# Moving the first turn of expert rows ahead of a top-k search, in a two-layer hybrid decoder kernel

## What is computed

```python
def peer(h, wq, keys, u_tab, v_tab):
    q = (xc @ wq).reshape(c, PEER_HEADS, 2, PEER_QDIM // 2)
    sc = jnp.einsum('thpd,hpkd->thpk', q, keys)
    top_v, top_i = lax.top_k(sc, PEER_TOPK)
    cand = (top_v[:, :, 0, :, None] + top_v[:, :, 1, None, :]).reshape(c, PEER_HEADS, -1)
    best_v, best_pos = lax.top_k(cand, PEER_TOPK)
    ids = jnp.take_along_axis(cand_id, best_pos, axis=-1)
    gate = jax.nn.softmax(best_v, axis=-1)
    act = jax.nn.gelu(jnp.einsum('td,thkd->thk', xc, u_tab[ids])) * gate
    return jnp.einsum('thk,thkd->td', act, v_tab[ids])

for layer in range(2):
    x = x + mixed(rms_norm(x, norm_mix[layer])) @ w_out[layer]
    x = x + peer(rms_norm(x, norm_ffn[layer]), ...)
```

## Time and profile before

| | us |
|---|---|
| median of 3 runs | 1578.69 (1577.34 to 1579.03) |
| the profiled execution | 1583.69 |
| its span in the profile | 1581.9 |
| PE busy | 1366.8 |
| DVE busy | 1173.6 |
| ACT busy | 455.0 |
| POOL busy | 608.3 |

### The profile page before, as it was taken

The page is one execution under the profiler, slowest core; times in us unless marked ns, Lnnn a source line. Parts: engine busy times, 40 slices in busy tenths (PEclk is TensorE's granted clock), DMA queues, the critical chain, the costliest instruction groups (busy, mean ns, idle before and its releaser), DMA issues.

```text
span 1581.9 us, 15174 instructions
## 1 busy us (share of the span) xinstructions
PE 1366.8 (86%) x4622; PEld 741.3 (47%) x4622; DVE 1173.6 (74%) x2848; ACT 455.0 (29%) x1095; POOL 608.3 (38%) x525
## 2 busy tenths in 40 slices
PE   8998999999695997988888799999969787788777
PEld 4766455554472444443356345455437433333333
DVE  6828999788698887874569788886658987665554
ACT  3522144443212234342122134343212222121112
POOL 1003355345334334553434333545434434333331
PEclk9999999999898999998989899999989889989999
DMA  9648999999999999999999999999999999999997
GB/s 360 269 164 347 389 380 422 406 402 421 423 421 421 422 398 422 422 419 423 423 410 409 422 423 420 417 384 403 422 423 419 388 408 422 422 419 421 422 421 300
DMA packets 87517, 629.97 MB, mean 398 GB/s; under 512 B 9825, under 2 KB 11105, under 8 KB 16910
## 3 DMA queue, kind: packets, MB, share of 16 engines
q0 software_dynamic: 74144, 537.97, 82.6%
q1 hardware_dynamic: 13294, 91.05, 14.1%
HBM read 627.91 MB, written 1.06 MB: 398 GB/s over the span
## 4 chain that ended last, share of the span: by engine, by line
PE 43%; DMA 29%; DVE 18%; issue 7%; ACT 3%; POOL 1%; SPq 0%; DVEq 0%; ACTq 0%
DMA ring<-table_uv,ids 28%; PE ps L1669 24%; DVE ring L1301 6%; PE ps L1636 5%; PE ps L1449 3%; PE ps L1412 2%; PE ps L1614 1%; ACT acts L797 1%; ACT diag L820 1%; PE ps L1516 1%; PE ps L1680 1%; POOL ring L1724 1%; DVE W L1276 1%; DVE W L1274 1%; DVE W L1277 1%
## 5 line engine op out<-in xcount | busy, mean ns | idle before, releaser
L1669 PE MATMUL ps<-ring,diag 128*128 128x512 f32 x1884 | 890.0, 627 | 194.3 <-ACT diag L820 185.4
L1724 POOL DMA_INDIRECT ring<-table_uv,ids x512 | 602.7, 1177 | 939.1 <-PE ps L1669 779.4
L1669 PEld LDWEIGHTS ps<-ring,diag 128*128 128x128 f32 x1884 | 370.7, 201 | 663.6 <-issue 652.0
L1301 DVE CUSTOM_DVE_ANT_0 ring<-ring,h 128x1024 f32<-128x1024 f32 x384 | 455.2, 1223 | 139.9 <-DMA ring<-table_uv,ids 137.9
L797 ACT ACTIVATE acts<-dots,small 128x4 f32<-128x4 f32 x126 | 37.5, 297 | 876.3 <-DVE dots L1301 850.3
L1301 DVE CUSTOM_DVE_ANT_0 ring<-ring,ps 128x1024 f32<-128x1024 f32 x120 | 144.6, 1220 | 97.7 <-DMA ring<-table_uv,ids 97.5
L820 ACT ACTIVATE diag<-cst,weights 128x128 f32<-128x128 f32 x471 | 151.4, 390 | 28.9 <-DVE weights L1310 27.8
L1449 PE MATMUL ps<-W,hT 128*128 128x512 f32 (+2 forms) x256 | 95.2, 527 | 2.7 <-DVE hT L940 2.7
L1636 PEld LDWEIGHTS ps<-hT,W 128*128 128x128 f32 x832 | 94.5, 192 | 3.3 <-issue 3.3
L1636 PE MATMUL ps<-hT,W 128*128 128x128 f32 x832 | 95.3, 275 | 0.0
L1449 PEld LDWEIGHTS ps<-W,hT 128*128 128x128 f32 x256 | 48.5, 190 | 52.0 <-issue 47.4
(11 more groups left out here) (316 smaller groups left out, 1190.8 us busy)
## 6 DMA issues: line engine op xcount, KB each, us to landing
W<-peer_wq SPq DMA_DIRECT2D x11, 2048.0 KB, 19.7
W<-w_in SPq DMA_DIRECT2D x16, 1282.0 KB, 11.6
W<-w_out SPq DMA_DIRECT2D x7, 2048.0 KB, 11.2
ring<-table_uv,ids POOLq DMA_INDIRECT x512
W<-w_in SPq DMA_DIRECT2D x8, 898.0 KB, 8.8
ring<-peer_wq SPq DMA_DIRECT2D x3, 2048.0 KB, 21.0
W<-w_in SPq DMA_DIRECT2D x4, 1024.0 KB, 11.5
ring<-w_in SPq DMA_DIRECT2D x2, 1544.0 KB, 20.3
```

The source lines that it names most:

```text
L1301: v.tensor_tensor_reduce(ring_u[:, r, :], ring_u[:, r, :], tokens, 1.0, 0.0, ALU.mult, ALU.add, dots[:, s:s + 1]).then_inc(dots_done, 1)
L1669: mm = pe.matmul(ps[:, c, :], diag[:, s, :], ring_v[:, r, c * 512:(c + 1) * 512], start=(k == 0), stop=(k == SLOTS - 1), skip_group_check= ...
L1724: gp.indirect_dma_start(ring[:, place(t), :], None, table_uv, bass.IndirectOffsetOnAxis(ap=ids[:, b, k:k + 1], axis=0)).then_inc(pair_in[p ...
```

## The change

- The list of steps: "best 5" and "pairs 5" leave their place ahead of turn 0 and stand behind turn 0's rows of v; "query 3" and "score 3", which stood ahead of those rows, stand behind them too (and behind best 5 and pairs 5). "project 0" moves from turn 3 to turn 2, "project 3" from turn 4 to turn 3.
- The ring: slots 8 to 11 take the places of slots 0 to 3, as soon as PE has used these, and slots 12 and 13 take the two places that wait for query 3. `before(t)` names the slot whose place slot t takes, `filled(t)` counts how often a place has been filled.
- PSUM: the scores of head 1 (step 5) go to bank 5 and no longer to bank 1, so turn 0's rows of v don't wait for best 5; score 3 waits for it instead. The four products of block 2's projection go to banks 6, 7, 2 and 3, so it waits for best 1 and no longer for best 3.

```diff
-FIRST_PLACE = 4
+PLACES = (4, 5, 6, 7, 8, 9, 0, 1)
+AGAIN = (4, 5, 6, 7, 2, 3, 8, 9, 0, 1)
...
-             ["quick 0", "best 4", "pairs 4", "query 5", "score 5", "query 1", "score 1", "ids 4", "query 2", "score 2", "best 5", "pairs 5",]]
+             ["quick 0", "best 4", "pairs 4", "query 5", "score 5", "query 1", "score 1", "ids 4", "query 2", "score 2"]]
...
-    inner = [["ids 5", "best 1"], ["rows 0", "best 2"], ["best 3"],
-             ["project 0", "project 1", "project 2", "pairs 1", "ids 1"],
-             ["project 3", "project 4", "project 5", "pairs 2"],
+    inner = [["ids 5", "best 1"], ["rows 0", "best 2"], ["project 0", "best 3"],
+             ["project 1", "project 2", "project 3", "pairs 1", "ids 1"],
+             ["project 4", "project 5", "pairs 2"],
...
-            if n == 0 and i == 0:
-                do(["query 3", "score 3"], n)
             if i == 0:
                 plan.append(("rows of v", n, i))
+            if n == 0 and i == 0:
+                do(["best 5", "pairs 5", "query 3", "score 3"], n)
...
-            return (t + FIRST_PLACE) % RING
+            return PLACES[t] if t < 8 else AGAIN[(t - 8) % RING]
+
+        def before(t):
+
+            return None if t < 8 or t in (12, 13) else t - 8 if t < 12 else t - RING
...
-            return (2, 3, 0, 1, 0, 1)[bank] if n == 0 or n == 1 and bank >= 4 else 2 + bank
+            return (2, 3, 0, 1, 0, 1)[bank] if n == 0 or n == 1 and bank >= 4 else (6, 7, 2, 3)[bank] if n == 1 else 2 + bank
...
-                    pe.wait_ge(sc_used, searched(n - 1, 3))
+                    pe.wait_ge(sc_used, searched(n - 1, 1 if n == 1 else 3))
...
-                bank = 1 if part[0] == 2 else 2 + q
+                bank = 5 if part[0] == 2 else 2 + q
+                if (n, q) == (0, 3):
+                    pe.wait_ge(sc_used, searched(0, 5))
...
-                        pe.wait_ge(sc_used, searched(0, 5))
...
-                        if t >= RING:
-                            m, j = (t - RING) // RING_G, (t - RING) % RING_G
+                        if before(t) is not None:
+                            m, j = divmod(before(t), RING_G)
...
-                        elif t >= 4 and t % 2 == 0:
-                            gp.wait_ge(qT_ps, t // 2)
+                        elif t in (4, 6, 12):
+                            gp.wait_ge(qT_ps, 4 if t == 12 else t // 2)
```

More of the change, by code:

```diff
@@ L448, in place, with filled @@
         def place(t):
-            return (t + FIRST_PLACE) % RING
+            return PLACES[t] if t < 8 else AGAIN[(t - 8) % RING]
+        def before(t):
+            return None if t < 8 or t in (12, 13) else t - 8 if t < 12 else t - RING
+        def filled(t):
+            return 1 if before(t) is None else filled(before(t)) + 1 if t < 14 + RING else filled((t - 14) % RING + 14) + (t - 14) // RING
         def found_ids(n, i):
@@ L1198, in best_scores @@
                     v.wait_ge(sc_ps, 4 * n + q + 1)
-                bank = 1 if i == 5 else 2 + q
+                bank = 5 if i == 5 else 2 + q
                 k0 = 12 if (n, i) == (0, 3) else 0
@@ L1297, in take_dots @@
                     s, r = g * RING_G + j, place(RING_G * m + j)
-                    v.wait_ge(pair_in[r], 16 * ((RING_G * m + j) // RING + 1))
+                    v.wait_ge(pair_in[r], 16 * filled(RING_G * m + j))
                     if m >= 2 and j == 0:
@@ L1321, in take_dot @@
                 m, s, r = HALVES * n + k // RING_G, k % HELD, place(SLOTS * n + k)
-                v.wait_ge(pair_in[r], 16 * ((SLOTS * n + k) // RING + 1))
+                v.wait_ge(pair_in[r], 16 * filled(SLOTS * n + k))
                 v.wait_ge(gelu_done, parts_done(m - 2))
@@ L1448, in project @@
                     c0, c1 = BANK_CUTS[i:i + 2]
-                    mm = pe.matmul(ps[:, 2 + i, 0:c1 - c0], hT[:, k, :], win_at(n)[:, slot, c0:c1], start=(k == 0), stop=(k == KC - 1))
+                    mm = pe.matmul(ps[:, z_bank(n, i), 0:c1 - c0], hT[:, k, :], win_at(n)[:, slot, c0:c1], start=(k == 0), stop=(k == KC - 1))
                     if k == KC - 1:
@@ L1662, in add_rows @@
                         pe.wait_ge(z_act, 6)
-                        pe.wait_ge(sc_used, searched(0, 5))
                 for j in range(own_slots(m)):
                     s, k, r = g * RING_G + j, RING_G * i + j, place(RING_G * m + j)
-                    pe.wait_ge(pair_in[r], 16 * ((RING_G * m + j) // RING + 1))
+                    pe.wait_ge(pair_in[r], 16 * filled(RING_G * m + j))
                     pe.wait_ge(diag_ready, by_pe(m) + j + 1)
@@ L1676, in add_row @@
                 r = place(t)
-                pe.wait_ge(pair_in[r], 16 * (t // RING + 1))
+                pe.wait_ge(pair_in[r], 16 * filled(t))
                 pe.wait_ge(diag_ready, by_pe(t // RING_G) + k % RING_G + 1)
```

## The result

| | before | after |
|---|---|---|
| median of 4 runs each, us | 1578.01 (1576.12 to 1579.03) | 1586.47 (1584.57 to 1588.31) |
| profiled execution, us | 1583.69 | 1584.57 |
| span, us; granted clock | 1581.9; 0.945 | 1582.8; 0.948 |

The change makes the kernel slower: the ratio is 1.0047, 95% interval 1.0032 to 1.0062, which is 5.0 to 9.8 us; the medians differ by 8.5 us. The two profiled executions differ by 0.9 us alone, and that misleads: the one of before lies 5.7 us over its median, the one of after is the fastest of its four. In before's profile PE reaches query 2 at 125.99 us, in all others at 122.93 to 124.19 us, although nothing ahead of it has changed. So I compare **places relative to the start of query 2** (the row of L1645, 64 products, at 123.33 us in after).

The account below looks back on a forecast made before the run. DVE's list up to turn 8 was taken to set the end, with the DMA the bound from 310 us; +8.28 us at best 1, carried through, gave 1578.69 + 8.3 = 1587.0 us, range 1583.5 to 1590.0 us.

Parts of the forecast that it names:

- The bound: DVE's list leads up to turn 8, PE starting 0.75 us behind its weights; what DVE loses there the end loses.
- Query 3 and the exponential: On ACT, query 3's copy comes late ahead of ids 5's exponential; DVE stands 6.6 us, best 1 starts 8.28 us late.
- The first stand: DVE ahead of turn 0's weights stands about 3.6 us for the gelu, against 1.70 us before.
- Turn 1's rows: On PE, they start 8.28 us later, at 164.6 us, and take 8.80 us as before.
- Kept to turn 8: DVE's whole +8.28 us at best 1 lasts to turn 8, whose rows start on PE at 245.75 us.
- From turn 8 to the end: The chain carries the shift to the dry stretch at 308 us, the DMA from 310 us on: +8.3 us.
- The ring: New places for gathers: slot 14 at about 166.4 us for 160.21, at no cost, as DVE hardly waits for gathers.
- The table load: On ACT ahead of turn 0's gelu: 1.28 us, next instruction 0.02 behind, on the path to turn 0's rows.
- Rival 1: Turn 0's rows on PE run at a lower clock, +1.9 us before query 3: 1588.9 us, chance 0.13.
- Rival 2: DMA, restarted by turn 5's rows, keeps less: only 5.9 us reach the end, 1584.6 us, chance 0.12.
- Rival 3: Ids 5's exponential isn't held; DVE loses about 2.0 us at turn 0's gelu: 1580.7 us, chance 0.08.
- Rival 4: PE leads up to turn 8 and gains 5.6 us from filled idle time: 1573.1 us, chance 0.07.

Follow-up runs that it names:

- pad_best1: The kernel before plus six DVE reductions with unused results (4.3 us together) ahead of best 1: ratio 1.0026.
- pad_turn13: The kernel before plus six DVE reductions with unused results (4.3 us together) behind turn 13's weights: ratio 0.9997.
- best5_old_chunks: best5_between with the chunks of block 2's projection put back in turns 3 to 5: ratio 1.0007.
- ids5_first: The changed kernel with ids 5 moved ahead of query 3 in the list: 1580.15 us, ratio 1.0004.
- tops_between_b: The same program as tops_between, run once more: 1576.47 us, ratio 0.9978.
- best5_between: The changed kernel with best 5 between turn 0's dots and weights, and pairs 5 and ids 5 ahead of query 3: 1578.18 us, ratio 0.9993.
- best5_between_b: The same program as best5_between, run once more: 1578.16 us, ratio 0.9990.
- tops_between: best5_between with the first four maximum operations of best 2 and best 3 between dots and weights of turns 1 and 2: 1575.24 us, ratio 0.9969.
- query3_late: The kernel before with only query 3 and score 3 moved behind turn 0's rows of v: 1593.32 us, ratio 1.0084.
- query3_late_ids5: query3_late with ids 5 moved ahead of query 3 in the list: 1587.54 us, ratio 1.0048.

## Why the prediction was right

Against query 2's start, which lay at 125.99 us in the profile that it was worked out from, its steps give:

| step | predicted | measured |
|---|---|---|
| turn 0's rows | 10.33 | 10.33 |
| query 3 | 17.27 | 17.28 |
| DVE's stands | 3.6 and 6.6 | 0.73 + 2.87 and 6.66 |
| best 1 | 27.47 | 27.48 |
| PE idle ahead of the transposes and turn 1 | about 6 and 5 | 6.48 and 3.79 |
| turn 1's rows, length | 8.80 | 9.82 |
| turn 2's rows | 50.5 | 51.33 |
| PE late at turn 4 | 5.9 | 6.8 |
| turn 8 | +8.28 | +7.92 |
| medians | +8.3 (1587.0 us) | +8.5 (1586.47 us) |

- **The bound.** In these two kernels DVE's list up to turn 8 sets the end. The waits and PE's start 0.75 us behind the weights said so, and pad_best1 and pad_turn13 showed it from both sides. With DVE early, PE can take over: best5_old_chunks.
- **Query 3 and the exponential.** The step on which all hangs was that ACT's list keeps its order while PE's changes. Its sum (one turn's rows, and turn 0's new start) gave query 3's place to 0.01 us. ids5_first took the cause away, and with it 7 of the 7.9 us.
- **The first stand.** I had the gathers in by 130.5 us and all of the stand on the gelu. One gather was 0.73 us late in the dots. It doesn't count, since the gelu came later still.
- **Turn 1's rows**, mis-sized: I took 8.80 us from the earlier trace rows for an idle time of 4.49 us; it was 9.82. With it PE was 6.8 us late at turn 4 (80.13 us behind query 2 for 73.37) and not 5.9. DVE's lateness is still the greater, so nothing of it reached turn 8. The idle time was no measure of the length: in pad_turn13 turn 1's rows took 9.93 us behind the same 4.49 us that gave 8.80 in before.
- **Kept to turn 8**: 0.37 us less than the shift of best 1. Before, DVE waited for PE once on the way, a row of DVE's timeline in the kernel before that the prediction left out as "as good as without a gap":

```profile
212.45 0.48 DVE L991 TENSOR_SCALAR h<-ps,small 128x256 f32<-128x256 f32 x1 [0.31 <-PE ps L1449]
```

  PE is less late there than DVE, so this wait is gone: 0.31 of the 0.37 us.
- **From turn 8 to the end.** The forecast has the whole shift carried on. The pair of profiles has 6.22 us at turn 15, as turn 14's rows were the slower ones in before, and 3.6 at the end; what takes the rest is not resolved, and single executions of one kernel differ by as much (1576.12 to 1579.03 us for before). That the shift is carried rests on the table of ratios. That the medians agree with the forecast to 0.2 us is chance, with an interval of 5.0 to 9.8 us.
- **The ring.** The prediction has slot 14's gather at about 166.4 us, 6.2 us later than before, though turn 1's rows, for which it waits, were put 8.28 us later. POOL issued it at 166.02 us in after, which is 42.69 us behind query 2 for 34.22 before: 8.5 us later. It cost nothing, as forecast, since DVE waited for no gather behind turn 0.
- **The table load.** The next instruction starts 0.01 or 0.02 us behind each load of 1.28 us (131.30 and 132.59, 148.56 and 149.86 us in ACT's rows above). The prediction's sum has 1.28 and 0.02 us for it, from the earlier trace rows, and best 1's shift came out at 8.29 us for 8.28.
- **The rivals.** Rival 1 didn't happen: turn 0's rows took 7.11 us behind 1.18. That it can happen is shown by tops_between_b, where they took 8.75 us behind 1.25, at a granted clock of 0.50 from 134 to 136 us (PE's timeline):

```profile
133.72 8.75 PE L1690 MATMUL ps<-ring,diag 128*128 128x512 f32 x16 [1.25 <-ACT diag L833]
```

  There the exponential doesn't wait for query 3, and turn 8 is where it was. In after it would be on the path; the spread of its runs, 3.7 us, may come of this, which no profile here shows. Rival 2 would have left 5.9 us, or 6.8 by what its PE term came out at, and the interval of the time, 5.0 to 9.8 us, excludes neither. best5_between speaks against it: there PE starts turn 5, from which this rival has the DMA restarted, at 204.83 - 122.96 = 81.87 us behind query 2 for 212.25 - 125.99 = 86.26, which is 4.4 us early, and the time is between 3.2 us earlier and 0.9 later (4.1 and 0.9 in best5_between_b). Rival 3 is the kernel ids5_first: not what the change does, but what it costs otherwise; its 2.0 us came out at 1.52 at best 1 and 0.88 at turn 8. Rival 4 has its condition, best 1 early, in best5_between, and even there PE's idle times give 1 to 2 us and not 5.6.

The prediction's 1578.69 us for before was 0.7 us over the median beside the kernel after. The profiled execution was forecast at about 1592 us on the ground that before's was 5 us over its median; that was no property of the kernel, and it came out at 1584.57 us.

## What to carry to other kernels

An order written for one engine moves the lists of the others too. When a product moves, look in the copying engine's list for what is queued behind its copy: here an exponential of 0.31 us behind a copy that came 8.3 us late cost 6.7 us of an engine that had no slack, and moving that step ahead of the product gave back 7.0 of the 7.9 us at turn 8. A turn can fill its own wait for an activation with a piece of a search that needs nothing from it: with turns 1 and 2's waits of 0.36 us filled, turn 8 came 1.0 us earlier in tops_between than in best5_between_b.

## What I hadn't expected of the hardware

- In after the rows of turns 2 to 8 took 7.0 to 7.1 us each, at a granted clock of 1.00 from 174 to 250 us. Up to 330 us the profiles have 12 turns whose rows stood behind an idle time of PE of 3.79 to 7.29 us, and these took 8.8 to 10.1 us: 9.82 behind 3.79 in after, 10.02 behind 4.00 in best5_old_chunks, 9.47 behind 5.20 in query3_late, 8.82 behind 5.19 and 9.19 behind 7.29 in query3_late_ids5. Their length didn't grow with the idle time. From 156 to 166 us in after, from the transposes to the first part of turn 1's rows, the granted clock was 0.50.
- Behind shorter idle times the same program had either length. Turn 6 of best5_between took 8.80 us behind 1.90 us (granted clock 0.50 from 216 to 218 us) and 7.11 behind 1.90 in best5_between_b (1.00); turn 0 took 7.11 behind 1.24 in tops_between and 8.75 behind 1.25 in tops_between_b, and turn 14 7.11 and 8.80 in the same two, both behind 1.56 us. Each of these places was worth 1.6 or 1.7 us, and the idle time ahead of it didn't say which. At turn 6 it moved turn 8 by 1.0 us; where it lies on the path, it may be part of the spread between runs, which no run here isolates.
